# A decoder step with retention: transposes in halves of the array's rows, and one f32 product in place of six split products

## The reference, cut to what matters

```python
def step(s, inp):
    qi, ki, vi = inp
    inner = jnp.einsum('bihd,bjhd->bhij', qi, ki) * decay_in
    o = jnp.einsum('bhij,bjhe->bihe', inner, vi)
    o = o + jnp.einsum('bihd,bhde->bihe', qi, s) * q_decay[None, :, :, None]
    s = s * chunk_decay[None, :, None, None] + jnp.einsum('bjhd,bjhe->bhde', ki * k_decay[None, :, :, None], vi)
    return s, o
...
o = ((o - mu) * lax.rsqrt(var + GN_EPS)).reshape(b, t, nv)
out = (jax.nn.silu(g) * o).astype(x.dtype) @ w_o
```

## Time and profile before

| what | value |
| --- | --- |
| median of 3 runs | 2904.94 us (2904.34 to 2904.95) |
| the profiled execution's own time | 2901.5 us |
| its span, first to last instruction | 2899.7 us |
| TensorE (PE) busy | 2829.5 us, 98% |
| VectorE (DVE) busy | 1481.2 us, 51% |
| ScalarE (ACT) busy | 905.7 us, 31% |
| GpSimd (POOL) busy | 597.3 us, 21% |
| mean granted TensorE clock | 0.990 of full speed |

### The profile page before, as it was taken

One profiled execution on the slowest core, in us unless ns is written; L12 is line 12 of the kernel. 1 busy time (PEld: TensorE's weight loads), 2 busy tenths in 40 slices (PEclk: granted clock), 3 DMA queues, 4 the chain that ended last, 5 costly groups with the idle time before them and its releaser, 6 DMA issues.

```text
span 2899.7 us, 44286 instructions
## 1 busy us (share of the span) xinstructions
PE 2829.5 (98%) x18132; PEld 2723.1 (94%) x18132; DVE 1481.2 (51%) x2974; ACT 905.7 (31%) x1686; POOL 597.3 (21%) x505
## 2 busy tenths in 40 slices
PE   8999989999999999999999999899999999999997
PEld 7888879999999999899999999899899999999996
DVE  5555576444444444614445354365675444444446
ACT  5445454211111222322443433422252212222113
POOL 3333351000000002402223232122230000000004
PEclk9999999999999999999999999999999999999998
DMA  4210011111111111134566565776402111111101
GB/s 132 78 45 17 30 45 44 45 44 49 54 44 44 44 59 51 64 118 148 185 190 191 187 189 176 241 229 200 138 30 73 44 44 44 58 45 44 44 25 59
DMA packets 193433, 260.49 MB, mean 90 GB/s; under 512 B 29200, under 2 KB 151696, under 8 KB 193200
## 3 DMA queue, kind: packets, MB, share of 16 engines
q1 hardware_dynamic: 128336, 196.16, 21.6%
q10 hardware_dynamic: 64896, 61.50, 6.2%
HBM read 191.50 MB, written 68.20 MB: 90 GB/s over the span
## 4 chain that ended last, share of the span: by engine, by line
PE 91%; DVE 4%; ACT 2%; DMA 1%; issue 1%; POOL 1%; SPq 0%; DVEq 0%; POOLq 0%; ACTq 0%
PE bank L493 29%; PE bank L495 28%; PE bank L494 28%; PE bank L628 1%; PE bank L648 1%; PE bank L638 1%; ACT y L1033 1%; PE bank L942 1%; PE bank L546 1%; DVE xl L1518 1%; DVE y L1491 1%; PE bank L905 0%; PE bank L890 0%; PE bank L605 0%; DVE bank L1503 0%
## 5 line engine op out<-in xcount | busy, mean ns | idle before, releaser
L493 PE MATMUL bank<-xh,wh 128*128 128x344 f32 x3624 | 1170.0, 323 | 12.3 <-DMA xl<-scratch_heads_lo 7.3
L495 PE MATMUL bank<-xh,wl 128*128 128x344 f32 x3624 | 1159.0, 320 | 0.0
L494 PE MATMUL bank<-xl,wh 128*128 128x344 f32 x3624 | 1158.7, 320 | 0.0
L493 PEld LDWEIGHTS bank<-xh,wh 128*128 128x128 f32 x3624 | 682.6, 188 | 27.9 <-issue 17.0
L494 PEld LDWEIGHTS bank<-xl,wh 128*128 128x128 f32 x3624 | 682.3, 188 | 5.1 <-issue 0.5
L495 PEld LDWEIGHTS bank<-xh,wl 128*128 128x128 f32 x3624 | 682.8, 188 | 0.0
L1481 DVE TENSOR_TENSOR y<-bank,y 128x344 f32<-128x344 f32 x576 | 290.4, 514 | 230.5 <-PE bank L495 229.8
L2126 POOL TENSOR_TENSOR f_hl<-f_cv,f_hh 128x344 fp32r<-128x344 f32 x132 | 123.0, 933 | 1266.6 <-ACT f_hh L1182 1266.6
L493 PE MATMUL bank<-f_hh,wh 128*128 128x344 f32 x1056 | 339.8, 322 | 0.0
L495 PE MATMUL bank<-f_hh,wl 128*128 128x344 f32 x1056 | 337.4, 319 | 0.0
L494 PE MATMUL bank<-f_hl,wh 128*128 128x344 f32 x1056 | 337.1, 319 | 0.0
(11 more groups left out here) (234 smaller groups left out, 3479.3 us busy)
## 6 DMA issues: line engine op xcount, KB each, us to landing
raw<-in_w SPq DMA_DIRECT2D x216, 512.0 KB, 3.7
scratch_qkvg<-p_plain ACTq DMA_DIRECT2D x96, 172.0 KB, 2.9
r_s<-in_state_in SPq DMA_DIRECT2D x32, 512.0 KB, 3.7
out_state_s<-r_s ACTq DMA_DIRECT2D x32, 512.0 KB, 5.5
scratch_qkvg<-p_rot ACTq DMA_DIRECT2D x24, 344.0 KB, 2.9
xh<-scratch_heads_hi SPq DMA_DIRECT2D x12, 688.0 KB, 8.4
xl<-scratch_heads_lo SPq DMA_DIRECT2D x12, 688.0 KB, 9.3
r_cxq<-scratch_qkvg SPq DMA_DIRECT2D x32, 256.0 KB, 5.6
```

The costliest lines, as they stand in the source:

```text
L493: pe.matmul(out, ah, bh, start=(k == 0), stop=False)
L494: pe.matmul(out, ah, bl, start=False, stop=False)
L495: mm = pe.matmul(out, al, bh, start=False, stop=(k == n - 1))
```

## The change

The values are turned in eight transposes in place of four: each 128x128 block is cut into its upper and its lower 64 rows, the upper half goes to bank 3 and the lower to bank 4 (now one tensor `K.two` over both banks), 64 columns each. The gated output's `back` is cut the same way. The keys' transposes move to the upper half of bank 3, and the product of keys and queries to the end of bank 4. That product is now two f32 matmuls on the loaded tile `r_cxq`, so the rounding and the low part are made for the queries alone. `back(i-1)` moves behind `update(i, 0)` on TensorE and its `gated` behind `update(i, 0)` on VectorE. As `back` now writes into bank 4 too, it waits for `inn` of the current chunk. VectorE's `rows` waits for `k_hi` ahead of both of its instructions.

```diff
+def halves(t):
+    return t.rearrange("p (j a n) -> p j a n", a=2, n=HD)
+def turned_halves(K):
+    return K.two[:, :, 0:RK].rearrange("p a (j n) -> p j a n", n=HD)
...
-        K.bank = [ctx.enter_context(nc.psum_tensor(f"bank{n}", [P, 512], F32)) for n in range(8)]
+        K.two = ctx.enter_context(nc.psum_tensor("bank34", [P, 2, 512], F32))
+        K.bank = [*low, K.two[:, 0, :], K.two[:, 1, :], *high]
...
# TensorE
         for j in range(2):
-            pe.transpose(inner_bank[:, j * W:(j + 1) * W], K.cxq[:, i % 2, 2 + j, :], ident[:, :])
+            pe.transpose(turned[:, RK + j * W:RK + (j + 1) * W], K.cxq[:, i % 2, 2 + j, :], ident[:, :])
         for j in range(4):
-            mm = pe.transpose(turned[:, j * W:(j + 1) * W], K.cxv[:, j, :], ident[:, :])
+            for half in range(2):
+                r = slice(HD * half, HD * half + HD)
+                mm = pe.transpose(K.two[:, half, HD * j:HD * j + HD], K.cxv[r, j, :], ident[r, r])
         mm.then_inc(R["turned"], 1)

     def inner(i):
-        pe.wait_ge(R["q_lo"], i + 1)
         pe.wait_ge(R["k_lo"], i + 1)
-        accumulate(pe, inner_bank[:, 2 * W:3 * W],
-                   [(K.qkh[:, 2 + j, :], K.qkl[:, 2 + j, :], K.qkh[:, j, :], K.qkl[:, j, :]) for j in range(2)])\
-            .then_inc(R["inner"], 1)
+        for j in range(2):
+            mm = pe.matmul(inner_bank[:, 3 * W:4 * W], K.cxq[:, i % 2, 2 + j, :], K.cxq[:, i % 2, j, :],
+                           start=(j == 0), stop=(j == 1))
+        mm.then_inc(R["inner"], 1)

     def back(i):
         pe.wait_ge(R["ga"], i + 1)
         if i + 1 < NI:
-            pe.wait_ge(R["v_lo"], i + 2)
+            pe.wait_ge(R["inn"], i + 2)
         for j in range(4):
-            mm = pe.transpose(turned[:, j * W:(j + 1) * W], K.ga[:, j * W:(j + 1) * W], ident[:, :])
+            for half in range(2):
+                r = slice(HD * half, HD * half + HD)
+                mm = pe.transpose(K.two[:, half, HD * j:HD * j + HD], K.ga[r, j * W:(j + 1) * W], ident[r, r])
         mm.then_inc(R["back"], 1)
...
         if live:
             inner(i)
+        if live:
+            update(i, 0)
         if 1 <= i <= NI:
             back(i - 1)
-        if live:
-            update(i, 0)
         fill(FILL[i][1])
...
# ScalarE, GpSimd: queries alone
-        act.activation(K.qkh[:, :, :], K.cxq[:, i % 2, :, :], ACT.Copy).then_inc(R["q_hi"], 1)
+        act.activation(K.qkh[:, :, :], K.cxq[:, i % 2, 0:2, :], ACT.Copy).then_inc(R["q_hi"], 1)
...
# VectorE
         dve.wait_ge(R["v_hi"], i + 1)
-        dve.tensor_tensor(K.vl[:, :], bank[3][:, :], K.vh[:, :].bitcast(F32), ALU.subtract).then_inc(R["v_lo"], 1)
         dve.wait_ge(R["k_hi"], i + 1)
+        dve.tensor_tensor(halves(K.vl[:, :]), turned_halves(K), halves(K.vh[:, :].bitcast(F32)), ALU.subtract)\
+           .then_inc(R["v_lo"], 1)
...
         if live:
             decayed(i)
+            update(i, 0)
         if 1 <= i <= NI:
             gated(i - 1)
         if live:
-            update(i, 0)
             inner_lo(i)
...
# SyncE: the load of queries and keys
-        after(sp, R["turned"], i - 1)
+        after(sp, R["inner"], i - 1)
```

More of the change, by code:

```diff
@@ L340, in build @@
         K.R = {n: ctx.enter_context(nc.semaphore("r_" + n)) for n in RET_SEMS}
-        K.bank = [ctx.enter_context(nc.psum_tensor(f"bank{n}", [P, 512], F32)) for n in range(8)]
+        low = [ctx.enter_context(nc.psum_tensor(f"bank{n}", [P, 512], F32)) for n in range(3)]
+        K.two = ctx.enter_context(nc.psum_tensor("bank34", [P, 2, 512], F32))
+        high = [ctx.enter_context(nc.psum_tensor(f"bank{n}", [P, 512], F32)) for n in range(5, 8)]
+        K.bank = [*low, K.two[:, 0, :], K.two[:, 1, :], *high]
         def place(at):
@@ L455, in build @@
         K.vh = sb("r_vh", [P, RV], F32R)
-        K.qkh = sb("r_qkh", [P, 4, W], F32R)
+        K.qkh = sb("r_qkh", [P, 2, W], F32R)
         sb = place(BASE + 4 * SLAB * (RAW + 6 + 4))
@@ L459, in build @@
         K.vl = sb("r_vl", [P, RV], F32R)
-        K.qkl = sb("r_qkl", [P, 4, W], F32R)
+        K.qkl = sb("r_qkl", [P, 2, W], F32R)
         with nc.Block() as block:
@@ L927, in output @@
         if n:
+            pe.wait_ge(R["q_lo"], i + 1)
             pe.wait_ge(R["s_lo"], rows_of_state(i))
@@ L1301, in values_hi @@
         after(act, R["out_"], i)
-        act.activation(K.vh[:, :], bank[3][:, :], ACT.Copy).then_inc(R["v_hi"], 1)
-        act.activation(K.kdh[:, :], bank[4][:, 0:RK], ACT.Copy, scale=K.dec[:, h % 2, W:W + 1]).then_inc(R["k_hi"], 1)
+        act.activation(halves(K.vh[:, :]), turned_halves(K), ACT.Copy).then_inc(R["v_hi"], 1)
+        act.activation(K.kdh[:, :], bank[3][:, RK:], ACT.Copy, scale=K.dec[:, h % 2, W:W + 1]).then_inc(R["k_hi"], 1)
     def queries_hi(i):
@@ L1854, in rows @@
         dve.wait_ge(R["v_hi"], i + 1)
-        dve.tensor_tensor(K.vl[:, :], bank[3][:, :], K.vh[:, :].bitcast(F32), ALU.subtract).then_inc(R["v_lo"], 1)
         dve.wait_ge(R["k_hi"], i + 1)
-        dve.scalar_tensor_tensor(K.kdl[:, :], bank[4][:, 0:RK], K.dec[:, h % 2, W:W + 1], K.kdh[:, :].bitcast(F32),
+        dve.tensor_tensor(halves(K.vl[:, :]), turned_halves(K), halves(K.vh[:, :].bitcast(F32)), ALU.subtract)\
+           .then_inc(R["v_lo"], 1)
+        dve.scalar_tensor_tensor(K.kdl[:, :], bank[3][:, RK:], K.dec[:, h % 2, W:W + 1], K.kdh[:, :].bitcast(F32),
                                  ALU.mult, ALU.subtract).then_inc(R["k_lo"], 1)
@@ L1861, in decayed @@
         dve.wait_ge(R["inner"], i + 1)
-        dve.tensor_tensor(K.inn[:, :], bank[4][:, 2 * W:3 * W], K.dec[:, i // NB % 2, 0:W], ALU.mult).then_inc(R["inn"], 1)
+        dve.tensor_tensor(K.inn[:, :], bank[4][:, 3 * W:4 * W], K.dec[:, i // NB % 2, 0:W], ALU.mult).then_inc(R["inn"], 1)
     def inner_lo(i):
@@ L1871, in gated @@
         after(dve, R["ob_lo"], i)
-        dve.tensor_tensor(K.ob[:, :, :], bank[3][:, :].rearrange("p (a n) -> p a n", a=4), K.cxg[:, i % 2, :, :], ALU.mult)\
-           .then_inc(R["ob"], 1)
+        dve.tensor_tensor(halves(K.ga[:, :]), turned_halves(K),
+                          K.cxg[:, i % 2, :, :].rearrange("p j (a n) -> p j a n", a=2), ALU.mult).then_inc(R["ob"], 1)
     def update(i, j):
@@ L2159, in queries_lo @@
         pool.wait_ge(R["q_hi"], i + 1)
-        pool.tensor_tensor(K.qkl[:, :, :], K.cxq[:, i % 2, :, :], K.qkh[:, :, :].bitcast(F32), ALU.subtract).then_inc(R["q_lo"], 1)
+        pool.tensor_tensor(K.qkl[:, :, :], K.cxq[:, i % 2, 0:2, :], K.qkh[:, :, :].bitcast(F32), ALU.subtract).then_inc(R["q_lo"], 1)
     def state_lo(i):
```

## The result

The changed kernel takes 2915.06 us (median of 8 runs, 2912.85 to 2916.66) against 2904.43 for the kernel before on the same chips (8 runs). The ratio is 1.0039, with a 95% interval of 1.0030 to 1.0048: **10.6 us slower** in the medians (8.7 to 13.9 by the interval), where +10.7 was forecast. The range held it.

The account below looks back on a forecast made before the run. TensorE, busy for 98% of the span, was taken to bound the kernel. The terms -5.8 + 9.6 - 1.1 - 0.15 + 8.2 gave +10.75, so 2915.6 us, range 2905 to 2924.

Parts of the forecast that it names:

- The transposes in halves: Values' and gated output's transposes on TensorE: 0.60 us a group instead of 0.45, two groups in 32 periods, +9.6 us.
- The high bound of 0.85: Upper bound for a group of half transposes if a pair's halves run one after the other: 0.85 us, +25.6 in all.
- The product: Product of keys and queries: two f32 matmuls take 0.44 us instead of 0.62 in each of 32 periods, -5.8 us.
- The new wait: `back` on TensorE waits for VectorE's `r_inn` in periods 2, 10, 18, 9, 17 and 25: +8.2 us.
- The wait for `k_lo`: In eight periods with VectorE late, `turn`'s extra time falls inside an existing wait; 0.14 us each given back, -1.1 us.
- Period 24: `turn`'s extra 0.15 us lies hidden before TensorE's wait for memory: -0.15 us.
- The clock: Rival: the new waits on TensorE lower the granted clock, once or a few times: 2919 to 2926 us; chance 0.14.
- The faster rival: Changing width costs these transposes nothing, a group takes 0.27 us: -7.7 us, 2897 us in all; chance 0.07.
- the serial halves: Rival: the halves of a pair run one after the other on TensorE: 2932 us; chance 0.08.
- halves at the old price: Rival: a group of half transposes costs 0.45 us like the full ones: +2.4, 2907 us; chance 0.09.
- no new wait: Rival: TensorE's wait for `r_inn` does not appear, needing `r_inn` a microsecond earlier: 2907 us; chance 0.06.

Follow-up runs that it names:

- run 2: The changed kernel with full 128x128 transposes in place of the halves, all else kept: ratio 1.0011 against the kernel before, +3.2 us.
- run 5: The changed kernel with only the upper halves, four half transposes a group instead of eight (output incomplete): ratio 1.0046 against the kernel before.
- run 6: The changed kernel with one pair of halves a group instead of four (output incomplete): ratio 1.0009 against the kernel before, +2.6 us.
- run 1: The kernel before with only the product of keys and queries as two f32 matmuls: 2898.55 against 2903.08 us, ratio 0.9986.
- run 3: The changed kernel with VectorE's order altered so `decayed` comes ahead of what held it up: ratio 1.0011 against the kernel before, +3.2 us.
- run 4: The changed kernel with each group's halves resequenced, four upper ones and then four lower ones: ratio 1.0044 against the kernel before.
- run 7: The changed kernel with the values' halves ahead of the keys' transposes in `turn`: ratio 1.0036 against the kernel before.

## Why the prediction was right, step by step

The mechanism came out as forecast in each of its terms, but that the medians agree to 0.1 us is luck: the interval is 5 us wide, and a term was missing. In the two profiles the retention, from the first transpose of `turn` to the last of `back`, takes 742.6 us before (1317.95 to 2060.54) and 755.9 after (1315.92 to 2071.78), 13.3 more. My sum did not hold 3.4 of them: 1.5 of low clock in period 25, and around the wait for memory 0.9 of a longer wait and 1.0 of low clock. The 9.9 that are left stand against the 10.75 of the sum; 0.5 of the difference is in the new wait and 0.3 in the one for `k_lo`. The rest of the execution is 2.0 us shorter ahead of the retention and 2.3 longer behind it, which cancels.

- **The transposes in halves, +9.6.** Forecast 0.60 a group against 0.45, measured 0.59 against 0.44. The estimate came from `sample_back`, which pays the same change of width, and from the pairs of the earlier trace rows. Shown by runs 2, 5 and 6. The high bound of 0.85 was added up wrongly: eight at 0.06 with 0.3 and 0.05 make 0.83, +24.3 and not +25.6.
- **The product, -5.8.** Forecast 0.44, measured 0.45 in run 1, whose median shows 4.1 (1.5 to 6.7). In the changed kernel the state's matmul is recorded 0.37 after the product's start and its successor 0.31 behind, where 0.23 is usual: 0.44 to 0.45 again, with part of it seen behind.
- **The new wait, +8.2.** Measured from the product's start, `back` begins at 2.33, 2.73 and 3.11 us in periods 2, 9 and 25 instead of at 1.25; that is 1.1, 1.5 and 1.9, where 1.08, 1.50 and 2.0 were forecast. The row says 7.7 in all, 0.5 under the forecast. The 8.1 that run 3 gives back are near the 8.2 by chance: they hold 1.5 of clock and lack the 1.0 passed on.
- **The wait for `k_lo`, -1.1.** Of its 0.20 only 0.02 is left in the changed kernel: the product begins 0.15 after the matmul before it in all eight periods, and takes 0.38 to the state's first matmul instead of 0.36. I had left 0.06 in each; the 0.3 us between are too little to be seen in a median.
- **Period 24, -0.15.** Can't be seen. The wait for memory itself was 7.3 us in the profile of before, 8.2 in that of after, and 7.6 to 8.8 in the others. What sets it was not looked into.
- **The clock, a rival at 0.14.** It came true at one wait of the six, and each time. Six profiles have waits for `r_inn`: the changed kernel and runs 2, 4, 5, 6 and 7. In all six the granted clock is 0.66 or 0.67 over the 5 us from the start of `back` in period 25, behind a wait of 1.8 to 2.0 us, and it does not fall behind any of the thirty shorter ones (1.0 to 1.6 us). In the five profiles without such waits it is 1.00 from 1890 to 2050 us. A window of run 6, and then one of run 3 (columns as above):

```profile
1904.77:1909.77 5.00, 5.00 (x23) 4.93 (x24) 2.65 (x6) 2.08 (x4) 1.29 (x1) 0.67 0.36 108
1890.00:2050.00 160.00, 160.00 (x1067) 146.68 (x1066) 93.18 (x191) 42.00 (x68) 31.00 (x21) 1.00 0.60 196
```

  So a lowered clock belongs to the new wait of period 25; whether by its length or by its place some 26 us behind the low clock of the memory wait, no run separates. Its price was too high in the prediction, which took 3.4 us from the earlier trace rows. The clock is also low while TensorE waits (in the changed kernel from 1875.6, 4.9 us before that wait ends), and that costs nothing. TensorE after the wait for memory, in the kernel before and then in the changed one:

```profile
1874.44 0.63 PE L493 MATMUL bank<-xh,wh 128*128 128x344 f32 x1 [7.26 <-DMA xl<-scratch_heads_lo]
...
1877.65 0.32 PE L495 MATMUL bank<-xh,wl 128*128 128x344 f32 x1
```

```profile
1880.53 0.62 PE L506 MATMUL bank<-xh,wh 128*128 128x344 f32 x1 [8.21 <-DMA xl<-scratch_heads_lo]
...
1885.82 0.33 PE L506 MATMUL bank<-xh,wh 128*128 128x344 f32 x1
```

  Eleven matmuls in 3.21 instead of 1.73, 1.5 us lost; and eighteen in 5.29 instead of 2.83, 2.5 lost. With 1.5 us instead of 3.4 for the one wait the rival's time comes to about 2917, inside the forecast's 2911 to 2920, and the medians cannot tell it from 2915.6.
- **The faster rival** (no price for the change of width) fell with run 6, **the serial halves** with run 5, **halves at the old price** with run 2, **no new wait** with the row of waits.

The Trainium skill, "TensorEngine Tiling (Array Packing)", gives up to 2x for a dimension of 64 or less (Theoretical Speedup); the trace agrees, halves on different rows do run two for one (run 5). It also says that a change of the tiling mode drains the engine (Key Properties); the draining itself is in no row, but the runs show 0.35 us a group for leaving and re-entering the full width, and that decides: it is more than the two for one gives back.

## What to carry to other kernels

Half-width transposes on a full engine save 0.05 us a block and cost 0.35 us for leaving and re-entering the full width: by these two numbers, an estimate, they need more than seven blocks in a row, or a neighbour of another shape already (run 7). Where a change lets one tensor span two banks, look at what the second bank's other user must finish first: a wait on an in-order engine costs what stands ahead of it there, and moving that behind brought back 8 us. A low clock is priced by the matmuls that run under it, and not by the length of the stretch. For products of 128 columns, price the records and not the passes: six split matmuls took 0.62 us, two f32 ones, four records 0.11 apart, 0.44 to 0.45. Whether such a record is held by its columns or by its weights no run separates.

## What the runs showed of the hardware that I had not expected

Matmuls on rows 0 to 63 and on rows 64 to 127 overlap even when four of the one kind are issued ahead of four of the other: 0.99 against 0.98 for the same distance (run 4). The order within a group does not have to alternate. I had taken the alternation of the earlier trace rows for a condition.

A wait of 1.8 to 2.0 us, with TensorE full before and after it, was followed by about 3.4 us at 1.2 GHz in six profiles out of six, and 30 waits of 1.0 to 1.6 us by none. I had given that a chance of 0.14.
